# Routing six of eight expert heads in the next block: a two-layer decoder with product-key experts on one Trainium2 core

## The chip, the cores and the metric

The kernel runs on one core of one Trainium2 chip. The metric is the device time of one execution in microseconds (us), lower is better. The core's engines are PE (matrix products), DVE (vector), ACT (activations), POOL (general purpose; here it only issues the gathers) and SP (here it only issues the plain loads). They run their own instruction streams in order and meet at semaphores. Data comes from device memory over 16 DMA engines that all queues share.

## What is computed

256 tokens of width 1024 go through two layers. Each layer is a mixer (layer 0: RWKV-7 and mLSTM heads; layer 1: causal attention with forget gates, 16 heads) and then a channel mixer, which is what this case is about:

```python
def peer_ffn(x, w_q, sub_k1, sub_k2, u_tab, v_tab):      # per block of 128 tokens
    q = (xb @ w_q).reshape(T, PEER_HEADS, 2, PEER_DHALF)           # 8 heads, halves of 128
    s1 = jnp.einsum('thd,hnd->thn', q[:, :, 0], sub_k1)            # 128 scores a half
    s2 = jnp.einsum('thd,hnd->thn', q[:, :, 1], sub_k2)
    v1, i1 = lax.top_k(s1, K)                                      # K = 16
    v2, i2 = lax.top_k(s2, K)
    cand = (v1[..., :, None] + v2[..., None, :]).reshape(T, PEER_HEADS, K * K)
    sc, ci = lax.top_k(cand, K)
    eid = e1 * PEER_NKEYS + e2                                     # e1, e2: i1, i2 at ci
    gate = jax.nn.softmax(sc, axis=-1)
    act = jax.nn.gelu(jnp.einsum('td,thkd->thk', xb, u_tab[eid]), approximate=False)
    return jnp.einsum('thk,thkd->td', gate * act, v_tab[eid])
```

Every token chooses 8 x 16 = 128 experts of 16,384, and needs a row of `u_tab` and one of `v_tab` (1024 float32 each) for each. Layer norms with a scaled residual stand between all parts.

## The kernel before

**Expert blocks.** There are four: n = 2 * layer + token block, so n = 0, 1 are layer 0 and n = 2, 3 layer 1. A *row* is one expert slot s (0 to 127) for all 128 tokens of a block: one indirect DMA of POOL (line 542) gathers 128 x 2048 float32, 1 MiB, into a slot of a ring of `RING = 11`. A row then goes through four engines: DVE forms the dot product with the token (line 1700), ACT makes GELU, gate weight and a diagonal matrix of the weights (lines 1201, 1206, 1214), PE adds diagonal times v row into PSUM (line 893), and only then is the ring slot free for POOL's next gather (`pe_rows`). PE does a pair of rows one pair later than DVE (`PE_LAG = 1`).

**Routing.** `route` (lines 1644 to 1687) is DVE's work of choosing experts, for a group of two heads at a time: top 16 of four score rows, the 256 sums, top 16 of those, the indices, the softmax. It has eight hooks (`meanwhile`), at which DVE may do pairs of rows. POOL waits for `experts_chosen` (line 535) before the first row of each head; ACT's exponential (`gates`, line 1227) stands in the middle of a group, and ACT's pairs of a head wait for its `gates_ready`.

**Which block runs beside what.** The rows of a block are spread over the mixer work of another by counts of pairs, the same on DVE, ACT and PE. Block n = 0 runs beside its own routing and that of n = 1. Block n = 1 (64 pairs) runs beside the layer-1 mixer of token block b = 0: 2 + 2 pairs at its start, 16 at the sixteen weight strips of the projections (`strip_pairs`), 2 + 16 in the attention, 4 at the output projection, 3 after the norm, 1 at the queries, and then in the *tail* (`mixer1_tail`, lines 968 to 1002 on PE, 1291 to 1318 on ACT, 1788 to 1799 on DVE) 12 beside the routing of n = 2: three hooks (`tail_pairs`) in each of four groups of heads. `finish` does the 6 that are left. Block n = 2 does the same beside b = 1 and the routing of n = 3. Block n = 3 runs by itself.

**Weights.** A strip is 1 MiB of a weight matrix, 256 columns, in a ring of three (`WRING = 3`), loaded by SP (line 430) once PE has filled the PSUM bank of the strip three before. The tail's query projection (`peer_q`, line 993) takes eight strips.

**Scores.** In the tail ACT copies the scores of each group of heads to `sc[:, 0]`, which lies in memory that the next block's attention uses for `SQ`, `lg` and `probT`.

Of the kernel before, what the change touches and what calls it, by code (L numbers as in the profile page):

```python
# [77 lines left out]
def tail_pairs(g, hook):  # L78

    return int(hook in (0, 2, 5))  # L80
# [8 lines left out]
def strip_pairs(i):  # L89

    return 1
# [107 lines left out]
def build(nc, T, out):  # L199
    ROWS, NROWS = parameter_rows()  # L200
    ctx = ExitStack()
    with ctx:
# [162 lines left out]
        keyT = cut(22528, 2048).rearrange("p (i n) -> p i n", i=16)  # L365
        qT = cut(24576, 4096).rearrange("p (i n) -> p i n", i=16)
        sc = cut(28672, 4096).rearrange("p (b i n) -> p b i n", b=NB, i=16)
        cand = cut(32768, 512).rearrange("p (h n) -> p h n", h=2)
        scr = cut(33280, 512)
        onehot = cut(33792, 512).rearrange("p (h k j) -> p h k j", h=2, k=TOPK)  # L370
        v16 = cut(34304, 64).rearrange("p (i k) -> p i k", i=4)
        i16f = cut(34368, 64).rearrange("p (h two k) -> p h two k", h=2, two=2)
        csc = cut(34432, 32).rearrange("p (h k) -> p h k", h=2)
        hilo = cut(34464, 64).rearrange("p (w h k) -> p w h k", w=2, h=2)
        e12 = cut(34528, 64).rearrange("p (w h k) -> p w h k", w=2, h=2)
        eidf = cut(34592, 32)
        gate = cut(34624, NB * SLOTS).rearrange("p (b s) -> p b s", b=NB)
        hid = cut(34880, NB * SLOTS).rearrange("p (b s) -> p b s", b=NB)
        ga = cut(35136, NB * SLOTS).rearrange("p (b s) -> p b s", b=NB)
        gsum = cut(35392, 2 * EH)  # L380
        uints = cut(35408, 416).bitcast(U32)
# [4 lines left out]
        diag = [cut(35840 + j * P, P) if j < 4 else early[:, (j - 4) * P:(j - 3) * P] for j in range(DIAGS)]  # L386
        qT1 = cut(24576, 2048).rearrange("p (i n) -> p i n", i=16)
# [3 lines left out]
        ogs = cut(24576, D)  # L391
        qc = cut(25600, 1024).rearrange("p (t n) -> p t n", t=8)
        kc = cut(26624, 2048).rearrange("p (t n) -> p t n", t=8)
        fv = cut(30720, 2048).rearrange("p (b n) -> p b n", b=NB)
        SQ = cut(28672, 2048).rearrange("p (t n) -> p t n", t=16)
        lg = cut(28672, 2 * 512).rearrange("p (j q n) -> p j q n", j=2, q=2)
        probT = cut(29696, 2 * 512).rearrange("p (j q s n) -> p j q s n", j=2, q=2, s=2)
        oT = cut(32768, D).rearrange("p (t n) -> p t n", t=KT)
# [21 lines left out]
        def _(sp):  # L420
# [32 lines left out]
            load_strips(16 + 3 - 3)  # L453
            await_filled(sp, "seq_y", NCH - 1)
            load_keys(0)
            load_strips(3)
# [95 lines left out]
        def _(pe):  # L552
# [415 lines left out]
            def mixer1_tail(b, ex):  # L968
# [16 lines left out]
                for g in range(GROUPS + 1):  # L985

                    def between(j):
                        for i in (range(0, 2), range(2, 4))[j]:
                            ex.pairs(tail_pairs(g - 1, i) if g else QUERY_PAIRS * (i == 0))

                    if g < GROUPS:
                        k = EH + 1 + 4 * b + g
                        feature_strips("peer_q", k, b, between)
                        pe.wait_ge(S("peer_q_taken"), k + 1)
                        ps = claim(pe, "peer_s", k).rearrange("p (q n) -> p q n", q=4)
                        done(score_keys(ps, 0, range(4 * g, 4 * g + 4), lambda j: qT1[:, j, :]), "peer_s")
                        first_hook = 4
                    else:
                        first_hook = 0
# [21 lines left out]
        def _(act):  # L1021
# [205 lines left out]
            def gates(n, groups, meanwhile):  # L1227

                for g, (h0, h1) in enumerate(groups):
                    for i in range(6):  # L1230
                        meanwhile(g, i)
                    gates_begun[0] += 1
                    act.wait_ge(S("gate_shifted"), gates_begun[0])
                    x = gate[:, n % NB, TOPK * h0:TOPK * h1]
                    af(x, x, ACT.Exp).then_inc(S("gate_exp"), 1)
                    for i in range(6, 8):
                        meanwhile(g, i)

            def mixer1(b, ex):
                tok = slice(b * P, (b + 1) * P)  # L1240
                wide = lambda ps: ps.rearrange("p (t n) -> p t n", n=P)
                take_x(4 + 4 * b, b)
                taken(af(fz, full(act, "fox_f", b)[:, 0:P], ACT.Identity, bias=small[:, 2:3], scale=1.0), "fox_f")
                ex.pairs(EARLY_PAIRS)
                for i in range(4):
                    ex.pairs(strip_pairs(2 * i))
# [9 lines left out]
                    ex.pairs(strip_pairs(2 * i + 1))  # L1256
                for i in range(2):
                    ex.pairs(strip_pairs(8 + 2 * i))
                    taken(copy(fv[:, b, i * 512:(i + 1) * 512], full(act, "fox_v", 2 * b + i)), "fox_v")
                    ex.pairs(strip_pairs(9 + 2 * i))  # L1260
                for i in range(12, 15):
                    ex.pairs(strip_pairs(i))
                for i in range(2):
                    taken(af(ogs[:, i * 512:(i + 1) * 512], full(act, "fox_og", 2 * b + i), ACT.Sigmoid), "fox_og")
                ex.pairs(strip_pairs(15))
# [610 lines left out]
```

## Time and profile before

| | us |
|---|---|
| median of 3 runs | 1821.57 |
| lowest, highest | 1821.03, 1824.02 |
| the profiled execution, its own time | 1815.61 |
| its span, first to last instruction | 1813.6 |

| engine | busy us | share of the span |
|---|---|---|
| PE | 1551.5 | 86% |
| DVE | 1063.3 | 59% |
| ACT | 606.0 | 33% |
| POOL | 576.3 | 32% |

DMA moved 638.32 MB: 536.90 MB of gathers (512 rows) and 100.24 MB of plain loads. On the page, the chain of work that ended last is 45% PE, 32% DMA and 15% DVE. The page's strips cut the span in 40 slices of 45.3 us. In the timelines a bracket behind an instruction gives the idle time of its engine before it and what ended it; the windows give each engine's busy time in a stretch, PE's granted clock (1.00 is the full one), the DMA engines' busy share and the rate at which they moved data.

### The profile page before, as it was taken

To read this page: it belongs to the slowest core of one execution; us is meant where nothing else is said; L and a number is where in the kernel's file an instruction comes from. 1 tells how busy PE (TensorE), PEld (TensorE's weight loads), DVE (VectorE), ACT (ScalarE), POOL (GpSimd) and SP (SyncE) were. 2 spreads that over 40 slices of the span, in tenths; PEclk is the share of its full clock that TensorE was granted. 3 is DMA by queue.
4 is the path that set the end of the run, shared out by engine and by line. 5 is a ranking of instruction groups with operands and counts; after the bars stand their busy time and mean duration, and the time that the engine had idled before them with its cause. 6 is when DMAs were issued, how large, how long until landed. Compare 5 with 4: busy or idle time off the path is not lost.

```text
span 1813.6 us, 18606 instructions
## 1 busy us (share of the span) xinstructions
PE 1551.5 (86%) x6020; PEld 927.1 (51%) x6020; DVE 1063.3 (59%) x2499; ACT 606.0 (33%) x1760; POOL 576.3 (32%) x561
## 2 busy tenths in 40 slices
PE   8999988998777778997899789998999787777775
PEld 7779877664222225753457436654557433222222
DVE  1683544577888865335557984325557985444444
ACT  1434311333333333236532332246632332222222
POOL 2000000344444442333332352234542354333330
PEclk9999859999999999999999999999999899999999
DMA  6222003999999999999999989999999899999996
GB/s 245 94 93 70 1 24 126 380 413 420 419 420 419 420 420 420 419 420 420 419 418 418 407 345 419 419 419 420 419 419 419 347 357 420 420 420 420 419 421 269
DMA packets 92063, 638.32 MB, mean 352 GB/s; under 512 B 11072, under 2 KB 13120, under 8 KB 15424
## 3 DMA queue, kind: packets, MB, share of 16 engines
q0 software_dynamic: 73728, 536.90, 71.9%
q1 hardware_dynamic: 18240, 100.24, 14.1%
q8 instruction: 49, 0.80, 0.2%
q14 instruction: 46, 0.38, 0.1%
HBM read 636.05 MB, written 1.05 MB: 351 GB/s over the span
## 4 chain that ended last, share of the span: by engine, by line
PE 45%; DMA 32%; DVE 15%; ACT 6%; issue 2%; POOL 0%; ACTq 0%; SPq 0%; DVEq 0%; POOLq 0%
DMA arena<-l_peer_uv,arena 31%; PE psum L893 19%; PE psum L575 12%; DVE arena L1700 6%; PE psum L874 4%; DMA wring<-l_w_in 2%; PE psum L752 1%; PE psum L797 1%; PE psum L668 1%; DVE arena L1639 1%; DVE arena L1630 1%; PE psum L658 1%; DVE arena L1631 1%; PE psum L667 1%; DVE arena L1635 1%
## 5 line engine op out<-in xcount | busy, mean ns | idle before, releaser
L542 POOL DMA_INDIRECT arena<-l_peer_uv,arena x512 | 563.1, 1100 | 1124.8 <-PE psum L893 870.2
L1700 DVE CUSTOM_DVE_ANT_0 arena<-arena,xres 128x1024 f32<-128x1024 f32 x512 | 617.8, 1222 | 454.8 <-DMA arena<-l_peer_uv,arena 452.3
L893 PE MATMUL psum<-arena,early 128*128 128x512 f32 x1024 | 487.9, 622 | 115.5 <-ACT early L1214 112.9
L893 PE MATMUL psum<-arena 128*128 128x512 f32 x1024 | 480.7, 615 | 100.5 <-ACT arena L1214 94.7
L893 PEld LDWEIGHTS psum<-arena,early 128*128 128x128 f32 x1024 | 193.6, 197 | 380.4 <-issue 205.4
L893 PEld LDWEIGHTS psum<-arena 128*128 128x128 f32 x1024 | 192.0, 195 | 360.0 <-issue 215.8
L575 PE MATMUL psum<-xT,wring 128*128 128x128 f32 (+2 forms) x1856 | 296.5, 320 | 13.8 <-DMA wring<-l_w_in 8.4
L575 PEld LDWEIGHTS psum<-xT,wring 128*128 128x128 f32 (+1 forms) x1856 | 269.2, 191 | 55.2 <-issue 23.2
L1201 ACT ACTIVATE arena<-arena 128x2 f32<-128x2 f32 x256 | 52.0, 203 | 646.7 <-DVE arena L1700 646.4
L1206 ACT ACTIVATE arena<-arena 128x1 f32<-128x1 f32 x512 | 123.2, 287 | 24.0 <-ACT arena L1201 0.4
L1029 ACT COPY arena<-psum 128x256 f32<-128x256 f32 (+2 forms) x138 | 62.5, 472 | 192.0 <-PE psum L575 85.9
L1214 ACT ACTIVATE arena<-ident,arena 128x128 f32<-128x128 f32 x256 | 86.9, 387 | 0.0
L1214 ACT ACTIVATE early<-ident,arena 128x128 f32<-128x128 f32 x256 | 86.9, 387 | 0.0
L874 PE MATMUL psum<-wring,xT 128*128 128x256 f32 x256 | 58.2, 380 | 0.3 <-DMA wring<-l_w_in 0.2
L874 PEld LDWEIGHTS psum<-wring,xT 128*128 128x128 f32 x256 | 48.4, 190 | 14.8 <-issue 6.2
L1201 ACT ACT_TABLE_LOAD x42 | 53.9, 1283 | 0.7
L1626 DVE MAX8 arena<-arena 128x8 f32<-128x128 f32 (+1 forms) x96 | 26.1, 326 | 38.3 <-ACT arena L1029 30.9
L1700 DVE DVE_READ_ACCUMULATOR2_ANT arena<- 128x1 f32 x512 | 42.1, 82 | 0.0
L1248 ACT ACTIVATE arena<-psum 128x512 f32<-128x512 f32 x8 | 4.8, 597 | 87.8 <-PE psum L575 87.8
L1782 DVE CUSTOM_DVE_ANT_0 arena<-psum,causal_ts 128x128 f32<-128x128 f32 (+1 forms) x32 | 10.2, 355 | 40.4 <-PE psum L943 40.4
L1630 DVE FIND_INDEX8 arena<-arena 128x8 uint32<-128x128 f32 (+1 forms) x96 | 31.5, 328 | 0.0
L752 PE MATMUL psum<-wring,arena 128*128 128x256 f32 x128 | 30.9, 404 | 0.7 <-DVEq L1602 0.7
(236 smaller groups left out, 1133.9 us busy)
## 6 DMA issues: line engine op xcount, KB each, us to landing
wring<-l_w_in SPq DMA_DIRECT2D x47, 1024.0 KB
wring<-l_peer_wq SPq DMA_DIRECT2D x24, 1024.0 KB
wring<-l_w_out SPq DMA_DIRECT2D x12, 1024.0 KB
arena<-l_peer_uv,arena POOLq DMA_INDIRECT x512
ln_par<-l_ln_g SPq DMA_DIRECT2D x6, 512.0 KB
ln_par<-l_ln_b SPq DMA_DIRECT2D x6, 512.0 KB
arena<-l_peer_keys SPq DMA_DIRECT2D x2, 1024.0 KB, 7.0
xT<-x_t SPq DMA_DIRECT2D x1, 1024.0 KB, 4.9
```

The source lines that it names most:

```text
L542: pool.indirect_dma_start(out=ring[:, g % RING, :], out_offset=None, in_=T[f"l{l}_peer_uv"], in_offset=bass.IndirectOffsetOnAxis(ap=eid[:, ...
L575: last = mm(ps, w[:, k, c0:c0 + cols], xT[:, k, tok], start=(k == 0), stop=(k == KT - 1))
L752: last = mm(ps[:, b * STRIP:(b + 1) * STRIP], yT[:, k, b * P:(b + 1) * P], w[:, k, :], start=first and (b, k) == (0, ks[0]), stop=end and ...
L874: last = mm(ps[:, i * STRIP:(i + 1) * STRIP], lhs(kt), w[:, kt, :], start=(kt == 0), stop=(kt == KT - 1))
L893: last = mm(self.ps[c], diag[k % DIAGS], ring[:, g % RING, D + c * 512:D + (c + 1) * 512], start=not self.begun, stop=True, skip_group_che ...
L1029: return nc.scalar.copy(out_, in_)
L1201: af(ga[:, self.b, 2 * p:2 * p + 2], hid[:, self.b, 2 * p:2 * p + 2], ACT.Gelu).then_inc(S("gelued"), 1)
L1206: af(w, w, ACT.Copy, scale=gate[:, self.b, s:s + 1]).then_inc(S("weights"), 1)
L1214: af(diag[k % DIAGS], ident[:], ACT.Copy, scale=ga[:, self.b, s:s + 1]).then_inc(S("diags_made"), 1)
L1626: st.then(v.max(vals[:, i, 0:8], src[:, i, :]))
L1630: st.then(v.max_index(idx[:, i, 0:8], vals[:, i, 0:8], src[:, i, :]))
L1700: v.tensor_tensor_reduce(out=u, in0=u, in1=xres[:, self.b, :], scale=1.0, scalar=0.0, op0=ALU.mult, op1=ALU.add, accum_out=hid[:, self.b, ...
```

## The change

Three things are edited.

1. The tail of a block routes only the first group of the next expert block (heads 0 and 1), now with six pairs at its hooks. PE's eight strips stand there with one pair after each of the last six, and ACT takes queries and scores between pairs. So 52 pairs are done when the tail ends instead of 58, and `finish` does 12 instead of 6.
2. The other three groups (heads 2 to 7) are routed while the next expert block runs: for n = 2 beside the sixteen strips of the next mixer, where DVE's 16 pairs now stand at 16 of the 24 hooks; for n = 3 right after the layer norm, with a pair at every one of 24 hooks. ACT's three exponentials move with them.
3. The scores must outlive the attention, so they get a buffer of their own, `sc1` (2048 columns), in the place of one ring row: `RING` is 10. All other addresses stay.

```diff
+FIRST_PAIR, LATER = PAIRS[:1], PAIRS[1:]
-RING = 11
+RING = 10
-def tail_pairs(g, hook):
-    return int(hook in (0, 2, 5))
+def tail_pairs(hook):
+    return int(hook in (0, 1, 2, 4, 5, 6))
+def routed_pairs(g, hook):
+    return int((8 * g + hook) % 3 != 2)
+def pairs_before_exp(g):
+    return sum(routed_pairs(j, i) for j in range(g + 1) for i in range(8 if j < g else 6))
...
+        sc1 = behind(0, 2048).rearrange("p (i n) -> p i n", i=16)
...
-                for g in range(GROUPS + 1):
-                    def between(j):
-                        for i in (range(0, 2), range(2, 4))[j]:
-                            ex.pairs(tail_pairs(g - 1, i) if g else QUERY_PAIRS * (i == 0))
-                    if g < GROUPS:
-                        k = EH + 1 + 4 * b + g
-                        feature_strips("peer_q", k, b, between)
...
-                    if g:
-                        for i in range(first_hook, 8):
-                            ex.pairs(tail_pairs(g - 1, i))
+                pumps = iter([QUERY_PAIRS, 0] + [1] * sum(tail_pairs(i) for i in range(8)))
+                for g in range(GROUPS):
+                    k = EH + 1 + 4 * b + g
+                    feature_strips("peer_q", k, b, lambda j: ex.pairs(next(pumps)))
...
+                held = LATER if b else ()
+                def strip_step(i):
+                    ex.pairs(strip_pairs(i))
+                    for g, (h0, h1) in enumerate(held):
+                        if pairs_before_exp(g) == i + 1:
+                            gate_exp(2, h0, h1)
...
-                    taken(copy(sc[:, 0, 4 * g:4 * g + 4, :], ps), "peer_s")
+                    taken(copy(sc1[:, 4 * g:4 * g + 4, :], ps), "peer_s")
...
-                gates(2 + b, PAIRS, meanwhile)
+                gates(2 + b, FIRST_PAIR, meanwhile)
...
             ex.pairs(NEW_PAIRS)
             ln_root(6)
+            gates(3, LATER, lambda g, i: ex.pairs(1))
             ex.finish()
...
+                def meanwhile(g, i):
+                    ex.pairs(routed_pairs(g, i))
+                    if (g, i) == (0, 4):
+                        decay_sizes()
+                if b:
+                    route(1, 0, LATER, meanwhile)
+                else:
+                    for i in range(16):
+                        ex.pairs(strip_pairs(i))
+                        if i == 2:
+                            decay_sizes()
...
-                route(1, b, PAIRS, lambda g, i: ex.pairs(tail_pairs(g, i)))
+                route(1, b, FIRST_PAIR, lambda g, i: ex.pairs(tail_pairs(i)))
...
             layer_norm(6)
+            route(1, 1, LATER, lambda g, i: ex.pairs(1))
             ex.finish()
```

On PE, in the tail of token block 0, from the second group of strips on. Line 575 is a strip of `peer_q`, 893 a row pair, 815 the scores of a group. Before:

```order
L575 MATMUL psum<-xT,wring 128x128 x16
L893 MATMUL psum<-arena 128x512 x4
L575 MATMUL psum<-xT,wring 128x128 x16
L893 MATMUL psum<-arena,early 128x512 x4
L815 MATMUL psum<-arena 128x128 x4
L893 MATMUL psum<-arena,early 128x512 x4
L575 MATMUL psum<-xT,wring 128x128 x16
L893 MATMUL psum<-arena 128x512 x4
L575 MATMUL psum<-xT,wring 128x128 x16
L893 MATMUL psum<-arena 128x512 x4
L815 MATMUL psum<-arena 128x128 x4
L893 MATMUL psum<-arena 128x512 x4
```

And in the changed kernel, where these lines are 588, 906 and 828:

```order
L588 MATMUL psum<-xT,wring 128x128 x16
L906 MATMUL psum<-arena 128x512 x4
L588 MATMUL psum<-xT,wring 128x128 x16
L906 MATMUL psum<-arena,early 128x512 x4
L828 MATMUL psum<-arena 128x128 x4
L588 MATMUL psum<-xT,wring 128x128 x16
L906 MATMUL psum<-arena,early 128x512 x4
L588 MATMUL psum<-xT,wring 128x128 x16
L906 MATMUL psum<-arena 128x512 x4
L828 MATMUL psum<-arena 128x128 x4
```

The pair behind each group's scores is gone: two pairs a group instead of three.

On DVE, at the end of the first routed group in the same tail (1681 to 1686 are its last operations, 1626 begins the next group, 1700 a row's dot product). Before:

```order
L1681 SCALAR_TENSOR_TENSOR arena<-arena 128x32
L1682 CAST arena<-arena 128x32
L1684 TENSOR_REDUCE arena<-arena 128x2
L1685 RECIPROCAL arena<-arena 128x2
L1686 TENSOR_TENSOR arena<-arena 128x32
L1626 MAX arena<-arena 128x8 x4
L1700 ISA arena<-arena,xres 128x1024
```

And in the changed kernel, where 1716 is the dot product; 24 rows follow, and then the layer norm:

```order
L1697 SCALAR_TENSOR_TENSOR arena<-arena 128x32
L1698 CAST arena<-arena 128x32
L1700 TENSOR_REDUCE arena<-arena 128x2
L1701 RECIPROCAL arena<-arena 128x2
L1702 TENSOR_TENSOR arena<-arena 128x32
L1716 ISA arena<-arena,xres 128x1024
L1716 ISA arena 128x1
```

Three groups of head routing have left this place.

## Rows read from the trace of the kernel before

**Rows 1.** The page's section 2: GB/s in 40 slices of 45.3 us.

```profile
GB/s 245 94 93 70 1 24 126 380 413 420 419 420 419 420 420 420 419 420 420 419 418 418 407 345 419 419 419 420 419 419 419 347 357 420 420 420 420 419 421 269
```

**Rows 2.** Windows: length; PE, PEld, DVE, ACT, POOL busy; clock, DMA share, GB/s.

```profile
440.00:640.00 200.00, 148.61 (x312) 58.00 (x312) 166.49 (x478) 61.17 (x210) 86.52 (x79) 0.97 1.01 420
...
1040.00:1072.00 32.00, 25.57 (x46) 10.37 (x45) 30.04 (x75) 12.88 (x43) 12.43 (x11) 0.82 0.82 304
...
1120.00:1200.00 80.00, 80.00 (x357) 54.42 (x356) 25.73 (x41) 18.51 (x69) 23.64 (x23) 1.00 1.01 419
...
1424.00:1480.00 56.00, 42.06 (x84) 17.70 (x83) 52.15 (x151) 20.05 (x62) 25.06 (x19) 0.85 0.84 309
...
1560.00:1760.00 200.00, 148.01 (x320) 57.49 (x320) 98.64 (x160) 50.68 (x201) 75.14 (x81) 1.00 1.01 420
```

**Rows 3.** DVE's timeline, two group starts; the tail's window for line 1700.

```profile
1011.64 0.87 DVE L1626 MAX8 arena<-arena 128x8 f32<-128x128 f32 x4
...
1034.24 0.86 DVE L1626 MAX8 arena<-arena 128x8 f32<-128x128 f32 x4
...
966.40:1056.80 90.40, 28.33 (x48) 0.92 0.98 398
```

**Rows 4.** POOL's gathers and a DVE dot product in the timeline of the first hole.

```profile
1042.59 0.94 POOL L542 DMA_INDIRECT arena<-l_peer_uv,arena  x1 [9.01 <-PE psum L893]
...
1066.53 1.50 POOL L542 DMA_INDIRECT arena<-l_peer_uv,arena  x1 [1.94 <-PE psum L893]
...
1072.86 1.23 DVE L1700 CUSTOM_DVE_ANT_0 arena<-arena,xres 128x1024 f32<-128x1024 f32 x1 [2.20 <-DMA arena<-l_peer_uv,arena]
```

**Rows 5.** Dots and loads by line, 944.7-1073.5/937-1073, then 1224.2-1479.3/1211-1475.

```profile
L1700 DVE CUSTOM_DVE_ANT_0 arena<-arena,xres x41: 1204/1221/1226, 944.8 to 1072.9; 128x1024 f32<-128x1024 f32 x41
L430 SPq DMA_DIRECT2D wring<-l_peer_wq x5: 328/328/1095, 964.0 to 995.2; - x5
L430 SPq DMA_DIRECT2D wring<-l_w_in x2: 337/385/433, 1013.6 to 1014.0; - x2
L430 SPq DMA_DIRECT2D wring<-l_w_in_rest x1: 555/555/555, 996.6 to 996.6; - x1
995.61 0.43 SPq L446 DMA_DIRECT2D ln_par<-l_ln_g  x1
L1700 DVE CUSTOM_DVE_ANT_0 arena<-arena,xres x86: 1204/1221/1236, 1224.3 to 1479.2; 128x1024 f32<-128x1024 f32 x86
L430 SPq DMA_DIRECT2D wring<-l_peer_wq x8: 327/380/912, 1328.6 to 1401.1; - x8
L430 SPq DMA_DIRECT2D wring<-l_w_out x3: 327/328/432, 1211.2 to 1328.2; - x3
1401.46 0.43 SPq L446 DMA_DIRECT2D ln_par<-l_ln_g  x1
```

**Rows 6.** Timelines of POOL and DVE early in block 0.

```profile
371.94 0.94 POOL L542 DMA_INDIRECT arena<-l_peer_uv,arena  x1 [8.01 <-PE psum L893]
...
378.14 1.22 DVE L1700 CUSTOM_DVE_ANT_0 arena<-arena,xres 128x1024 f32<-128x1024 f32 x1
...
380.87 1.23 DVE L1700 CUSTOM_DVE_ANT_0 arena<-arena,xres 128x1024 f32<-128x1024 f32 x1 [1.50 <-DMA arena<-l_peer_uv,arena]
```

**Rows 7.** PE's timeline in the tail: a strip, a pair of rows, the scores.

```profile
973.03 3.84 PE L575 MATMUL psum<-xT,wring 128*128 128x128 f32 x32 [0.27 <-DMA wring<-l_peer_wq]
976.70 3.60 PE L893 MATMUL psum<-arena,early 128*128 128x512 f32 x8
980.14 1.05 PE L815 MATMUL psum<-arena 128*128 128x128 f32 x8
```

**Rows 8.** One row's dot product on DVE, and the gather that its release lets go.

```profile
1147.30 1.23 DVE L1700 CUSTOM_DVE_ANT_0 arena<-arena,xres 128x1024 f32<-128x1024 f32 x1 [2.20 <-DMA arena<-l_peer_uv,arena]
...
1171.58 0.94 POOL L542 DMA_INDIRECT arena<-l_peer_uv,arena  x1 [4.23 <-PE psum L893]
```

More of the change, by code:

```diff
@@ L372, in build @@
[L372 to L379, printed above, removed]
@@ new lines, in build @@
+        onehot = behind(13312, 512).rearrange("p (h k j) -> p h k j", h=2, k=TOPK)
+        v16 = behind(13824, 64).rearrange("p (i k) -> p i k", i=4)
+        i16f = behind(13888, 64).rearrange("p (h two k) -> p h two k", h=2, two=2)
+        csc = behind(13952, 32).rearrange("p (h k) -> p h k", h=2)
+        hilo = behind(13984, 64).rearrange("p (w h k) -> p w h k", w=2, h=2)
+        e12 = behind(14048, 64).rearrange("p (w h k) -> p w h k", w=2, h=2)
+        eidf = behind(14112, 32)
+        gate = behind(14144, NB * SLOTS).rearrange("p (b s) -> p b s", b=NB)
@@ L382, in build @@
+        hid = behind(14400, NB * SLOTS).rearrange("p (b s) -> p b s", b=NB)
+        ga = behind(14656, NB * SLOTS).rearrange("p (b s) -> p b s", b=NB)
+        gsum = behind(14912, 2 * EH)
+        uints = behind(14928, 416).bitcast(U32)
         i16 = uints[:, 0:64].rearrange("p (i k) -> p i k", k=TOPK)
@@ L385, in build @@
         eid = uints[:, 160:416].rearrange("p (b s) -> p b s", b=NB)
[L386 to L398, printed above, removed]
+        diag = [behind(15360 + j * P, P) if j < 4 else early[:, (j - 4) * P:(j - 3) * P] for j in range(DIAGS)]
+        qT1 = behind(4096, 2048).rearrange("p (i n) -> p i n", i=16)
+        ogs = behind(4096, D)
+        qc = behind(5120, 1024).rearrange("p (t n) -> p t n", t=8)
+        kc = behind(6144, 2048).rearrange("p (t n) -> p t n", t=8)
+        fv = behind(10240, 2048).rearrange("p (b n) -> p b n", b=NB)
+        SQ = behind(8192, 2048).rearrange("p (t n) -> p t n", t=16)
+        lg = behind(8192, 2 * 512).rearrange("p (j q n) -> p j q n", j=2, q=2)
+        probT = behind(9216, 2 * 512).rearrange("p (j q s n) -> p j q s n", j=2, q=2, s=2)
+        oT = behind(12288, D).rearrange("p (t n) -> p t n", t=KT)
         fz, fl, fc = mr[:, 0, 0:P], mr[:, 0, P:SEQ], mr[:, 1, :]
@@ L452, in _ @@
             load_ln(0)
-            load_strips(16 + 3 - 3)
+            load_strips(16 + WRING - 3)
             await_filled(sp, "seq_y", NCH - 1)
             load_keys(0)
-            load_strips(3)
+            load_strips(6 - WRING)
             load_ln(2)
@@ L1245, in mixer1 @@
                 for i in range(4):
-                    ex.pairs(strip_pairs(2 * i))
+                    strip_step(2 * i)
                     ps = wide(full(act, "fox_qk", 4 * b + i))
@@ L1305, in take_scores @@
                     ps = full(act, "peer_s", EH + 1 + 4 * b + g).rearrange("p (q n) -> p q n", q=4)
-                    taken(copy(sc[:, 0, 4 * g:4 * g + 4, :], ps), "peer_s")
+                    taken(copy(sc1[:, 4 * g:4 * g + 4, :], ps), "peer_s")
+                taking = iter([(take_queries, 1), (take_scores, 1), (take_queries, 2), (take_scores, 2), (take_queries, 3),
+                               (take_scores, 3)])
                 def meanwhile(g, i):
-                    ex.pairs(tail_pairs(g, i))
-                    if g + 1 < GROUPS and i == 1:
-                        take_queries(g + 1)
-                    if g + 1 < GROUPS and i == 3:
-                        take_scores(g + 1)
+                    if tail_pairs(i):
+                        ex.pairs(1)
+                        take, g = next(taking)
+                        take(g)
                 ex.pairs(QUERY_PAIRS)
@@ L1746, in mixer1, with decay_sizes @@
             def mixer1(b, ex):
-                for i in range(2):
-                    ex.pairs(strip_pairs(i))
-                dve.wait_ge(S("fox_f_taken"), b + 1)
-                stt(fl, fz, -1.0, fz, ALU.mult, ALU.max).then_inc(S("f_abs"), 1)
-                for i in range(2, 16):
-                    ex.pairs(strip_pairs(i))
+                def decay_sizes():
+                    dve.wait_ge(S("fox_f_taken"), b + 1)
+                    stt(fl, fz, -1.0, fz, ALU.mult, ALU.max).then_inc(S("f_abs"), 1)
+                def meanwhile(g, i):
[9 more added lines that the diff above has]
+                            decay_sizes()
                 ex.pairs(RMS_PAIRS)
```

46 lines of the change are left out of this document (21 added, 25 removed).

## The prediction

> **What bounds the kernel now.** Read the page's GB/s line first [rows 1]: from slice 8 (363 us) on it stands at 418 to 421, with two holes, slices 22 and 23 (407, 345) and slices 31 and 32 (347, 357). The windows say the same at closer range: the DMA engines are busy 1.01 of the time and move 420 GB/s in the stretch of block 0 (440 to 640 us), 419 beside the mixer's strips (1120 to 1200) and 420 where block 3 runs alone (1560 to 1760); between 1040 and 1072 us they move 304, between 1424 and 1480 us 309 [rows 2]. So from 363 us to the last row the bytes of gathers and weights set the time, and only those two holes are open to gain. A row of 1 MiB costs 1.0486 MB / 420 GB/s = 2.50 us, a pair 5.0, a strip another 2.5.
>
> What makes a hole: POOL's gathers there wait for PE's line 893, that is for a ring slot to come free, once for 9.01 us [rows 4]. PE's rows wait for DVE. In the first hole DVE is busy for 30.04 of 32 us [rows 2]. It routes: one group of two heads takes 1034.24 - 1011.64 = 22.6 us [rows 3] and lets 3 pairs pass. In that time DMA needs 6 rows and 2 strips = 8 x 2.50 = 20.0 us. The ring covers the shortfall for about three groups, then DMA has nothing queued. At the end DVE has a stock of landed rows that it works off at 1.22 us a row, until it waits for DMA again at 1072.86 [rows 4].
>
> **Term 1, the holes.** By bytes: 32 x (420 - 304) / 420 = 8.8 us and 56 x (420 - 309) / 420 = 14.8 us, together 23.6 [rows 2]. But the end hangs on when whole rows have landed, and a row has landed when the last of 16 engines is through, so a second count goes from one dot product that waited for its row to the next such one [rows 5]. First hole: 41 dots from 944.77 to 1072.86 us are 40 rows; 5 + 2 strips and half a strip (the rest of w_in) are issued between, one more was under way, and the norm's parameters are another MiB: 49.5 MiB x 2.50 = 123.8 us in 128.1 us, 4.3 idle. Second: 85 rows, 11 strips, 1 for the norm: 97 x 2.50 = 242.5 us in 254.8 us, 12.3 idle. Together 16.6. The bounds are thus 16.6 and 23.6; I take **20**, between them, since either count has a reason and no row decides.
>
> **What the change does to the tail.** DVE: a group without its rows costs 22.6 minus its share of line 1700, 28.33 / 4 = 7.1, so 15.5 us [rows 3]; its six rows are that 7.1. With six pairs it costs 15.5 + 14.2 = 29.7 us, and DMA needs 12 x 2.50 = 30.0 us for the rows alone and another 20 for eight strips. DVE is no longer late: the 12 pairs left are then taken as they land. That removes the cause of both holes. Who is late next is PE. A strip costs it about 3.7 us, a pair 3.6, the scores 1.05 [rows 7]. A group of two strips with two pairs is 7.4 + 7.2 + 1.05 = 15.7 us, against 4 rows and 2 strips = 15.0 us of DMA. Three such groups fall behind by 2 us, and the rows stand behind two strips of which the last is loaded only once the bank three strips before it is full. Bounds for the idle time that this makes: 0, if what the ring holds covers it, and 5 us a tail (the 2 us and one wait such as the 2.5 us that a strip's own transfer takes). The second tail starts with less in the ring, so I take 1 us there and 0 in the first.
>
> **What it does to the next mixer (n = 2).** DVE gets 3 x 15.5 = 46.5 us of routing. The sixteen strip steps need 16 x 3 x 2.50 = 120 us of DMA, and DVE is busy there 25.73 of 80 us [rows 2], some 39 of 120; with the routing 85 of 120. It fits. No row shows routing in this stage, so from both sides: it costs nothing as long as a dot that comes late by the routing between two pairs does not hold PE. That is at most about 6 us: 15.5 us over eight hooks is 1.9 each, and up to three such pieces stand together where hooks have no pair. PE is busy 80.00 of 80 us here and runs behind DVE: the row dotted at 1147.30 freed its slot for the gather at 1171.58, 24 us later [rows 8], of which the dot is 1.2 and the pair's matmuls 3.6 [rows 7]. ACT's part is in the rest, but with PE never idle most of it is standing in line before PE; I count 15 us as cover for the 6, so the cost is 0. If the cover were gone, 16 pairs late by up to 2.9 us each are the 46.5. PE's strips wait for nothing new. ACT's three exponentials stand before a pair of strips each and wait for DVE's shifted scores; behind them on ACT stand the squares and copies of the attention's queries, and PE waits for these only when four banks later. DVE in its turn waits for the exponential at the end of a group, where ACT has just come from a PSUM bank of PE's: one or two us, under the same cover.
>
> POOL is held at the first row of heads 2 and 3, row 32. It may ask for it when row 22 is released; DVE has these heads chosen with 10 pairs done, 20 rows. So `experts_chosen` never holds a gather, nor for later heads (15 pairs done, row 64 wanted after 54).
>
> **Block 3.** Three groups with 8 pairs each: 15.5 + 16 x 1.18 (28.33 us / 24 rows, [rows 3]) = 34.4 us of DVE against 16 x 2.50 = 40 us of DMA. The trace has just this: block 0 beside the routing of block 1, DVE 166.49 of 200 us busy and 420 GB/s [rows 2]. Cost 0. The last rows, the layer norm and the store are as before.
>
> **The ring of ten.** With ten slots row r is asked for when row r + 1 was before. That matters only where a row came close. With an empty queue a gather needs 1072.86 - 1066.53 = 6.3 us from issue to dot [rows 4]. Early in block 0 the gather issued at 371.94 was dotted at 380.87, and the one before it would now be issued at 371.94 and is wanted at 378.14: 6.2 us [rows 6]. So it is tight but just in time there, with a strip under way besides. Elsewhere the ring loses one row of eleven. Bounds 0 and 2.5 us at each of about four places where PE is held up by other work (that one, the end of each attention, the start of the mixer). I take 1 us in all.
>
> By the Trainium skill, "DMA: Bandwidth & Descriptors", the section on the anatomy of a DMA by the GpSimd path, such a transfer takes 2.0 us plus its bytes at 436 GB/s, an estimate of 4.4 us for a row, and by that the ring would have 2 us more to spare at every tight place and cost nothing. The trace does not agree (6.3 us with the issue), so its figure is used.
>
> **The sum.** -20 + 1 + 1 = **-18 us**. Against the profiled execution's own 1815.6 us (1.99 us outside the span stay) that is 1797.6. It lay 6.0 us under the median of the runs; the same step below 1821.6 gives **1803.6 us**, 0.99 of before.
>
> **The rivals.**
> *A part of the hole stays (1811).* In the tail PE is the late one by 5 us each time, and the ring of ten loses 2.5 us at two places: of the 18 us gained 7 to 12 are given back, say 1811. For it: PE's 15.7 against 15.0 us, and that gathers are now asked for later. Against: PE has 1.4 us a pair to spare in the 12 pairs that follow.
> *All bytes come back (1798).* The GB/s count is the right one: -23.6. It is the low end of the range.
> *Nothing is gained (1820).* The idle time only moves: DVE's stalls in the mixer make the 15 us of cover vanish and the holes open there, about as large. It needs PE to lose its backlog; PE busy 80.00 of 80 us speaks against it.
> *Slower (1850).* The routing stands in series in the mixer of n = 2. One mechanism: DVE routes, a landed row waits, PE has no backlog, each strip step gets longer than 7.5 us. Price 3 x 15.5 = 46.5 less 18, so 1850. It begins where a row's whole turn (landing, DVE, ACT, PE, release, new gather) exceeds ten rows' worth of this stage, 10 x 3.75 = 37.5 us: 24 us after the dot and 6.3 to land are 31, and up to 6 of routing make 37. That is near, which is why the case has a chance at all; but the 24 us are mostly backlog and shrink when DVE is late.
> The Trainium skill has a rule that speaks for this side: "SBUF — State Buffer", section on the two separate sides, says that while DVE runs certain copies GpSimd is locked out of a port and cannot write the descriptors of its DMAs, so that the DMA starves. In the windows POOL is busy 86.52 us for 79 gathers beside routing and 75.14 us for 81 without [rows 2], 0.17 us more for each, and DMA stays at 420. For the 64 rows or so beside moved groups that is 11 us of POOL's time, none of it on the path.
>
> **Chances.** Forecast and its neighbour at 1798: 0.72. Part of the hole stays: 0.16. Nothing gained: 0.07. Slower: 0.05. What a measurement of this kernel can tell from no change is about 0.2%, 3.6 us: faster 0.88, same 0.07, slower 0.05. The range from 1797 to 1812 holds the first two cases, with the bounds of term 1 and the costs of ring and PE.
>
> **What would show it.** In the changed kernel's GB/s line the two holes are gone and no slice between 363 us and the last row is under 410. DVE's dots of n = 1 and n = 2 wait for DMA right after the single group in the tail. In the mixer of token block 1 DVE is busy some 28 of 40 us and GB/s stays at 419. The first gather of heads 2 and 3 waits for PE and not for DVE. Wrong would be: POOL waiting for DVE's line of chosen experts; PE idle for ACT's diagonals between strips; a hole at 1390 to 1420 us, where PE works off strips in the second tail.

## The result

| | us |
|---|---|
| before, median of 4 runs (range) | 1821.30 (1819.67 to 1824.02) |
| changed, median of 4 runs (range) | 1805.45 (1804.22 to 1809.39) |
| ratio, with its 95% interval | 0.9915 (0.9895 to 0.9936) |
| the profiled execution of the change, its span | 1806.65, 1804.5 |

The change saves 15.9 us; 18 were forecast. The repeats below gave 0.9928 (0.9913 to 0.9942) and 0.9912 (0.9893 to 0.9931), 13.8 and 16.0 us, so the three medians put the saving at 14 to 16 us.

### The profile page after: what moved, and what is told of

It reads as the page before. It is cut to its first block, busy times and chain, and to the rows that moved or that the text cites. A ratio compares the mean times of both kernels' runs of the same rounds, so it can differ in the third digit from the quotient of the medians.

```text
span 1804.5 us, 18617 instructions
## 1 busy us (share of the span) xinstructions
PE 1544.5 (86%) x6020; PEld 925.0 (51%) x6020; DVE 1063.3 (59%) x2499; ACT 604.9 (34%) x1759; POOL 579.8 (32%) x561
## 4 chain that ended last, share of the span: by engine, by line
PE 49%; DMA 37%; DVE 6%; ACT 5%; issue 2%; POOL 1%; ACTq 0%; SPq 0%; POOLq 0%; DVEq 0%
DMA arena<-l_peer_uv,arena 34%; PE psum L906 21%; PE psum L588 14%; PE psum L887 4%; DVE arena L1716 3%; DMA wring<-l_w_in 2%; PE psum L765 1%; DMA wring<-l_peer_wq 1%; PE psum L681 1%; PE psum L810 1%; PE psum L671 1%; PE psum L680 1%; ACT L1203 1%; POOL arena L555 1%; ACT early L1216 1%
## 5 line engine op out<-in xcount | busy, mean ns | idle before, releaser
L906 PE MATMUL psum<-arena,early 128*128 128x512 f32 x1024 | 477.8, 611 | 105.8 <-ACT early L1216 105.8
L906 PEld LDWEIGHTS psum<-arena,early 128*128 128x128 f32 x1024 | 189.4, 193 | 365.4 <-issue 194.6
L588 PE MATMUL psum<-xT,wring 128*128 128x128 f32 (+2 forms) x1856 | 296.5, 320 | 13.6 <-DMA wring<-l_w_in 8.4
L1031 ACT COPY arena<-psum 128x256 f32<-128x256 f32 (+2 forms) x138 | 62.5, 471 | 222.6 <-PE psum L588 125.8
L1647 DVE MATCH_REPLACE8 arena<-arena 128x128 f32<-128x128 f32 (+1 forms) x96 | 30.7, 320 | 0.0
L1456 DVE SCALAR_TENSOR_TENSOR arena<-psum,pars,arena 128x255 f32<-128x255 f32 x14 | 6.8, 482 | 40.2 <-ACT arena L1055 40.2
```

The costliest lines, as they stand in the source:

```text
L588: last = mm(ps, w[:, k, c0:c0 + cols], xT[:, k, tok], start=(k == 0), stop=(k == KT - 1))
L906: last = mm(self.ps[c], diag[k % DIAGS], ring[:, g % RING, D + c * 512:D + (c + 1) * 512], start=not self.begun, stop=True, skip_group_che ...
L1031: return nc.scalar.copy(out_, in_)
L1647: st.then(v.match_replace(scratch[:, i, :], vals[:, i, 0:8], src[:, i, :], -BIG))
```

## The profile after

Engines' busy time from the page's first section, then its GB/s line in 40 slices of 45.1 us, to be laid beside [rows 1]:

```profile
PE 1544.5 (86%) x6020; PEld 925.0 (51%) x6020; DVE 1063.3 (59%) x2499; ACT 604.9 (34%) x1759; POOL 579.8 (32%) x561
...
GB/s 246 95 92 72 1 11 130 342 390 419 419 420 419 420 420 413 419 419 420 419 415 419 414 420 416 420 419 420 419 378 419 405 420 421 419 420 420 420 419 260
```

DVE's total is the same to the tenth: no work was saved, only moved. The two deep holes of before (407, 345 and 347, 357) are gone. Three shallow ones are there: 390 in slice 8, 378 in slice 29, 405 in slice 31. The page's chain of work that ended last is now 49% PE, 37% DMA and 6% DVE, where DVE had 15%. The windows of the changed kernel (length; PE, PEld, DVE, ACT, POOL busy; clock, DMA share, GB/s) give first the place of the old first hole, then the new ones at close range:

```profile
1040.00:1072.00 32.00, 23.81 (x51) 9.24 (x50) 14.80 (x24) 7.72 (x30) 12.96 (x13) 0.97 1.01 420
376.00:384.00 8.00, 8.00 (x20) 3.56 (x19) 5.39 (x16) 4.48 (x19) 4.90 (x5) 1.00 0.80 264
1320.00:1328.00 8.00, 8.00 (x31) 5.54 (x30) 2.19 (x4) 2.47 (x10) 1.88 (x2) 1.00 0.62 224
1328.00:1336.00 8.00, 8.00 (x31) 5.54 (x30) 5.96 (x10) 1.50 (x7) 3.38 (x2) 1.00 1.00 374
1416.00:1424.00 8.00, 7.73 (x24) 3.82 (x23) 7.51 (x16) 5.84 (x19) 4.31 (x4) 1.00 0.97 376
1424.00:1432.00 8.00, 8.00 (x20) 3.61 (x19) 3.67 (x7) 2.14 (x9) 5.36 (x6) 1.00 0.98 385
```

Where [rows 2] had DVE busy for 30.04 of 32 us and 304 GB/s, DVE now is busy for 14.80 and the DMA engines for all of it. DVE's timeline in the first tail shows the turn. It finishes its one group, waits for ACT's exponential, works off five landed rows, and from then on waits for DMA before every row:

```profile
1014.02 0.19 DVE L1700 TENSOR_REDUCE arena<-arena 128x2 f32<-128x32 f32 x1 [8.28 <-ACT arena L1242]
...
1014.55 1.22 DVE L1716 CUSTOM_DVE_ANT_0 arena<-arena,xres 128x1024 f32<-128x1024 f32 x1
...
1019.13 1.22 DVE L1716 CUSTOM_DVE_ANT_0 arena<-arena,xres 128x1024 f32<-128x1024 f32 x1
...
1021.21 1.22 DVE L1716 CUSTOM_DVE_ANT_0 arena<-arena,xres 128x1024 f32<-128x1024 f32 x1 [0.85 <-DMA arena<-l_peer_uv,arena]
...
1072.21 1.23 DVE L1716 CUSTOM_DVE_ANT_0 arena<-arena,xres 128x1024 f32<-128x1024 f32 x1 [1.27 <-DMA arena<-l_peer_uv,arena]
1074.70 1.23 DVE L1716 CUSTOM_DVE_ANT_0 arena<-arena,xres 128x1024 f32<-128x1024 f32 x1 [1.26 <-DMA arena<-l_peer_uv,arena]
```

The last two stand 2.49 us apart, one row at the full rate. The 8.28 us are a new wait, three rows long. The rows that piled up were worked off at 1.15 us each, and DMA moved 406 and 410 GB/s in the two windows of 8 us from 1008 us on, so the wait cost half a us of bytes at most.

Now the next mixer. First for the kernel before, its window of 1080 to 1200 us and DVE's longest sum of waits in it (us in total, times, longest); then both for the changed kernel:

```profile
1080.00:1200.00 120.00, 116.43 (x518) 77.25 (x517) 48.44 (x78) 31.07 (x107) 38.47 (x36) 0.97 1.01 420
```

```profile
DVE arena L1700 <- DMA arena<-l_peer_uv,arena: 70.9, 31, 3.8
```

```profile
1080.00:1200.00 120.00, 114.44 (x518) 76.46 (x518) 84.92 (x254) 36.97 (x113) 38.80 (x34) 0.99 1.01 418
```

```profile
DVE arena L1716 <- DMA arena<-l_peer_uv,arena: 34.6, 21, 3.8
```

The routing went into time in which DVE waited for DMA: 36.5 us more work in this window, 36.3 us less waiting, and still 34.6 us to spare.

**Stretch by stretch.** The dot products of line 1716 (1700 before) are counted through, 512 of them; row 217 is the first that waits in the tail's approach to the first hole, row 348 the first dot product in the second tail's routing, row 384 the first of block 3. Times from one to the next, us, one trace of each kernel:

| kernel | first gather at | to row 44 | 44 to 217 | 217 to 256 | 256 to 264 | 264 to 348 | 348 to 384 | 384 to end |
|---|---|---|---|---|---|---|---|---|
| before | 321.0 | 136.3 | 492.1 | 123.4 | 20.7 | 279.5 | 106.1 | 334.5 |
| changed | 324.4 | 139.3 | 490.9 | 120.1 | 19.9 | 279.8 | 94.9 | 335.1 |
| a1_changed | 321.0 | 136.5 | 491.7 | 120.0 | 20.0 | 279.2 | 94.9 | 335.7 |
| c1_changed | 327.0 | 138.6 | 491.3 | 120.1 | 19.9 | 279.3 | 95.1 | 335.5 |
| a2_ring11 | 327.1 | 136.1 | 491.2 | 121.3 | 19.9 | 279.3 | 95.1 | 335.7 |
| c2_ring11 | 324.6 | 136.2 | 492.1 | 120.1 | 20.0 | 279.3 | 95.2 | 335.7 |
| a3_old_ring10 | 324.6 | 138.9 | 491.5 | 126.6 | 19.9 | 278.2 | 108.5 | 335.2 |
| a4_ring9 | 321.1 | 139.0 | 492.8 | 120.0 | 20.0 | 279.4 | 97.1 | 334.5 |
| b1_only_first | 323.5 | 136.2 | 492.1 | 120.1 | 20.0 | 279.4 | 109.1 | 335.0 |
| b2_only_second | 324.3 | 136.3 | 492.3 | 125.8 | 20.0 | 279.0 | 96.3 | 333.9 |
| b3_routing_plus_31 | 323.8 | 136.2 | 492.1 | 120.0 | 19.9 | 280.8 | 95.1 | 336.6 |
| b4_routing_plus_62 | 324.5 | 138.6 | 491.4 | 120.0 | 19.9 | 307.9 | 95.7 | 333.9 |

From the first gather on, the changed kernel's trace is 12.6 us shorter than that of before: 3.0 lost up to row 44, 1.2 won behind it, 15.0 won from row 217 to 384 (3.3 in the first hole, 0.8 behind it, 11.2 in the second, -0.3 between), 0.6 lost at the end. The span shrank by only 9.1, because the first gather came 3.5 us later, in layer 0, which the change does not touch. The "first gather at" column moves between 321 and 327 us in code that is the same up to there. Of the 7.7 us between the spans of the three traces of the changed kernel (1799.2 to 1806.9), 6.0 lie ahead of the first gather. The profiled execution of before was an early one.

## The experiments

Each carries a ratio to runs of the kernel before on the same chip. Their medians there were 1818.17 for the a set, 1818.82 for b and 1819.91 for c.

**Is the ring's lost row part of the price?** The changed kernel again, with eleven rows, with nine, and the old order with ten. With eleven rows the scores of all four groups lie elsewhere, in memory that costs no ring row; otherwise only the number of rows changes, and all other addresses stay.

```diff
-RING = 10
+RING = 11
...
+        def scores1(g):
+            if g == 0:
+                return sc[:, 0, 0:4, :]
+            if g < 3:
+                return masks[:, 512 * (g - 1):512 * g].rearrange("p (i n) -> p i n", i=4)
+            return mr[:, 4:6, :].rearrange("p r (i n) -> p (r i) n", i=2)
```

> The changed kernel again, as the yardstick for the kernels timed beside it. Both theories: ratio to before 0.991, some 16 us less. Holes in the DMA rate at about 376 to 384 us and 1320 to 1328 us, of 3 and 4 us.

Measured: 1804.42 us, 0.9928 (0.9913 to 0.9942). The hole at 1320 us came again (378 in slice 29), the one at 376 us did not (415 GB/s in that window).

> The moved routing with all eleven ring rows: the scores of heads 2 to 7 lie in tiles that layer 1 leaves unused (1024 columns of the masks, 512 of the small rows), so no ring row is given up. Theory 1 (the ring of ten costs 7 us, at 376 and at 1320 us, because a gather issued one release later comes late): 7 us less than the changed kernel, ratio to before 0.987, both holes gone, the small one at 1416 to 1432 us smaller. Theory 2 (what idle time is left comes from the new order of work, or from the start of the run): within 2 us of the changed kernel.

Measured: 1801.27 us, 0.9913 (0.9898 to 0.9928), 3.1 us less than a1: under half of what theory 1 said, and a little over theory 2. Of the two holes the one at 376 us is gone (394 GB/s) and the one at 1320 us is not (396 in slice 29).

> The kernel before with ten ring rows and nothing else. Theory 1: the same two new holes (3 and 4 us) and up to 2.5 us more in each old one: 7 to 12 us slower than before, ratio 1.004 to 1.007. Theory 2: no difference, under 2 us.

Measured: 1820.30 us, 1.0016 (1.0002 to 1.0030), 2.1 us more than before. Theory 1 named 7 to 12 and two new holes, of which only the one at 376 us came (255 GB/s; 417 in slice 29); the median lies just over theory 2.

> The changed kernel with nine ring rows, all else in place. Theory 1: each place where PE is held up loses 2.5 us more, and places that just held with ten begin to lose (starts of the mixers, the second tail): 12 to 20 us slower than the changed kernel. Theory 2: the ring is no limit, under 5 us slower.

Measured: 1807.02 us, 0.9948 (0.9933 to 0.9962), 2.6 us more than a1, as theory 2 said.

The changed kernel with eleven rows seemed 3.1 us faster, in a trace that is not shorter from the first gather on (1478.7 against 1478.2 us). So the pair was run once more.

> Repeat, beside the next kernel, of the changed kernel: ratio 0.9928 as measured in the first set.

Measured: 1803.91 us, 0.9912 (0.9893 to 0.9931).

> Repeat of the moved routing with all eleven ring rows. The first set gave 3 us less than the changed kernel by the medians, with intervals that touch, and no difference from the first gather to the end of the two traces. If the eleventh row is worth what the medians said: again 2 to 4 us less, ratio 0.991. If the traces are right: within 1.5 us of the changed kernel.

Measured: 1805.10 us, 0.9925 (0.9907 to 0.9943).

Now eleven rows were 1.2 us slower, within the 1.5 us that stood for the traces being right. The two pairs give 1 us in the mean for the eleventh row, with 3.1 and -1.2 apart: less than these runs can tell. In the table it seems to show in one place: up to row 44 all three traces with eleven rows take 136.1 to 136.3 us, while of eight with ten rows four take 138.6 to 139.3. Where such a trace shows a hole, it is in the window at 376 us above; three traces with eleven rows are too few to be sure of it. Nine rows cost 2.6 us by medians whose intervals overlap, and the table shows 2.2 us in the second tail, 97.1 instead of 94.9.

The hole at 1320 us is not the ring's. Slice 29 reads 360 to 396 in all nine traces with the first tail moved, with nine, ten and eleven rows, and 416 to 419 in the three without.

The old order reacts otherwise. With ten rows its first hole grew from 123.4 to 126.6 us and its second from 106.1 to 108.5, and these are its windows at the two holes, against 304 and 309 GB/s in [rows 2]:

```profile
1040.00:1072.00 32.00, 20.77 (x34) 8.51 (x35) 31.35 (x95) 10.56 (x34) 8.08 (x8) 0.79 0.78 302
1424.00:1480.00 56.00, 39.91 (x88) 17.87 (x87) 54.66 (x175) 19.19 (x58) 14.99 (x14) 0.79 0.80 302
```

A ring row is stock for the time in which DVE falls behind. With one row less the stretch of each open hole is 2.4 to 3.2 us longer, about one row's 2.5 us, here and in b1 and b2 below. Where the holes are closed, the tails show no such loss from eleven rows to ten. The medians are less sharp: the lost row costs 2.1 us in the old order, with an interval that reaches to 5.5, and 1 us in the new one. (The trace of a3 is 6.4 us longer from the first gather on, but it is of one of its slower executions, 1825.94 us, and 2.6 us of that lie ahead of row 44.) So that the row was dear in the old kernel and is nearly free in the new one is what the stretches say; the medians don't contradict it and don't prove it.

**Which half does it?** One tail keeps the old order with all four groups in it, the other has the new one. Both have ten rows.

```diff
+MOVED = (0,)
...
-                held = LATER if b else ()
+                held = LATER if b and 0 in MOVED else ()
...
-                pumps = iter([QUERY_PAIRS, 0] + [1] * sum(tail_pairs(i) for i in range(8)))
+                if b in MOVED:
+                    pumps = iter([QUERY_PAIRS, 0] + [1] * sum(tail_pairs(i) for i in range(8)))
...
+                for g in range(GROUPS + 1):
```

> Ten rows; only the first tail (token block 0) hands six heads on to the next mixer, the second routes all eight in place as before. Theory rows (a hole costs what the landings of whole rows lose: 3.4 us in the first, 12.6 in the second): 3 us gained less what the ring gives up (3 us in the kernel before with ten rows): ratio 0.998 to 1.002. Theory bytes (a hole costs the bytes not moved, 8.8 and 14.8 us): 8.8 less 3, ratio 0.997.

Measured: 1818.09 us, 0.9997 (0.9982 to 1.0012). That is theory rows; the 0.997 of theory bytes lies outside the interval.

> Ten rows; only the second tail hands six heads on, to block 3 which runs by itself. Theory rows: 12.6 us gained, less up to 3 for the ring in the first hole: 10 to 12 us, ratio 0.993 to 0.9945, nearly all that the whole change brings. Theory bytes: 14.8 less 3, and clearly less than the whole change.

Measured (`MOVED = (1,)`): 1810.13 us, 0.9947 (0.9929 to 0.9966), 8.7 us less than before: somewhat under both theories, and within the interval it can't tell them apart.

GB/s of both, first b1, then b2:

```profile
GB/s 244 94 93 70 1 24 116 370 414 419 420 419 420 419 420 407 419 420 420 419 416 417 413 420 419 419 420 419 420 378 419 336 348 420 421 419 420 420 420 272
```

```profile
GB/s 245 94 94 71 1 23 119 349 415 419 419 420 419 420 419 397 419 420 419 420 420 419 414 332 420 419 419 420 419 416 419 397 420 420 420 420 420 420 420 267
```

Each half closes its own hole and leaves the other, which is now deeper (336 and 348 for 347 and 357; 332 for 345), as in a3, whose ring is as short (341 and 353; 339). The stretches add up. Against the old order with ten rows the first tail is worth 126.6 - 120.1 = 6.5 us and the second 108.5 - 94.9 = 13.6; against eleven rows 3.3 and 11.2. Moving the first alone wins 3.3 us, loses 3.0 in the second hole (109.1 for 106.1) and so comes out at nothing. The first half of this change, tried alone, would have looked worthless. What no run separates is the routing from PE's new order in the same tail: both moved together each time.

**How near is the mixer's limit?** The rival "slower" said that the routing would stand in series there. To find the point from which that is so, DVE does more routing at the same place: the top 16 of each moved group's score rows are taken two or four times more, with the same values.

```diff
+                    for _ in range(2 if extra else 0):
+                        top16(sc1[:, js, :], scratch[:, 0:2 * nh, :], v16[:, 0:2 * nh, :], i16[:, 0:2 * nh, :], 2 * nh,
+                              lambda: None)
```

> The changed kernel; in the mixer of block 2 each of the three groups does the top 16 of its four score rows twice more (same values again), 5.2 us each time by the durations of the rows, 31 us of DVE in all. Theory cover (DVE has 120 - 85 = 35 us free there and PE's backlog hides when a dot comes late): 0 to 3 us slower than the changed kernel. Theory series (the moved routing is on the path in this stage, and what the holes gave was partly spent there): 15 to 31 us slower.

Measured: 1806.28 us, 0.9928 (0.9908 to 0.9949).

> The same with four repeats, 62 us more of DVE: more than the stage has free. Theory cover: now DVE sets the stage; 147 us of work against 120, 20 to 35 us slower than the changed kernel. Theory series: 62 us slower.

Measured: 1834.66 us, 1.0087 (1.0069 to 1.0104).

DVE's busy time on the two pages is 29.6 and 58.4 us above the changed kernel's 1063.3:

```profile
PE 1545.0 (86%) x6020; PEld 923.5 (51%) x6020; DVE 1092.9 (61%) x2691; ACT 605.3 (34%) x1759; POOL 579.0 (32%) x561
```

```profile
PE 1548.3 (85%) x6020; PEld 926.1 (51%) x6020; DVE 1121.7 (61%) x2883; ACT 605.3 (33%) x1759; POOL 583.2 (32%) x561
```

Both came out as theory cover had it. The first 29.6 us cost about nothing: the ratio is that of a1, and rows 264 to 348 take 280.8 us for 279.2 to 279.8 in the changed kernel and its repeats. The next 28.8 cost 27.1 us in the same stretch. Windows, first of b3, then of b4:

```profile
1120.00:1160.00 40.00, 39.76 (x205) 27.61 (x204) 36.15 (x147) 14.40 (x45) 10.71 (x12) 1.00 1.01 419
1160.00:1200.00 40.00, 37.58 (x126) 24.13 (x125) 38.60 (x157) 10.09 (x30) 11.49 (x12) 0.96 1.01 419
```

```profile
1120.00:1160.00 40.00, 31.09 (x164) 21.57 (x164) 39.10 (x155) 11.62 (x35) 9.90 (x9) 0.91 0.85 331
1160.00:1200.00 40.00, 31.58 (x116) 20.10 (x115) 38.94 (x178) 9.86 (x29) 9.52 (x9) 0.87 0.89 359
```

In b3 DVE is busy for up to 38.60 of 40 us and DMA still runs at 419: this is the edge. In b4 DVE is full, and the wait goes round: DVE is late, so ACT's diagonals are, so PE's rows, so POOL's gathers. These are one wait of PE and one of POOL in b4's timelines, and DVE's waits for DMA, which are nearly gone (34.6 us in the changed kernel):

```profile
1134.61 5.31 PE L906 MATMUL psum<-arena,early 128*128 128x512 f32 x8 [8.90 <-ACT early L1216]
...
1138.47 0.94 POOL L555 DMA_INDIRECT arena<-l_peer_uv,arena  x1 [15.13 <-PE psum L906]
```

```profile
DVE arena L1719 <- DMA arena<-l_peer_uv,arena: 7.7, 5, 2.2
```

So the rival's mechanism exists, its place is right, and its point is where DVE's own work fills the stage. 84.9 + 58.4 = 143.3 us of work against 120 us of DMA leaves 23 us in series; 28.1 were measured over the changed kernel's 279.8, and the runs don't say where the other 5 come from. The change stands some 30 us of DVE work on the near side of it.

## Why the prediction was right, and where not

**The bound and what lifts it: right in the main.** DVE's routing made the holes, and with one group in each tail they close; b1 and b2 show it hole by hole. The time is inside the range, 1.9 us above the number. By the stretches, 15.0 us come from rows 217 to 384, that is from the two places named. Two readings were too simple. Slice 8 of [rows 1] stands at 413, not at 418 or more. And DMA does not set the time everywhere from 363 us on: from row 331 to row 348, at the end of the attention and in the output projection, the dot products take 64.4 to 64.9 us in before, changed, a3, b1 and b2 alike, whether or not DMA has a hole there, and PE is busy for 24.00 of 24 us from 1320 to 1344 us in before and in the changed kernel.

That the number came so near is in part luck. From the first gather on, the traces of the changed kernel are 12.6, 12.7 and 14.4 us shorter than the one of before: the holes gave less than forecast (15.3 for 20), the start of block 0 could lose more (3.0 for 1), and up to 3.3 us of the medians' difference stand in no stretch.

**Term 1, the size: too large.** This is the term that was mis-sized: 20 us forecast, 15.3 measured. Two counts stood for the two holes, 23.6 us by missing bytes and 16.6 by landed rows, and 20 was taken between them because "no row decides". The stretches say 3.3 + 0.8 + 11.2 = 15.3 us, with what the ring and the new order give back in it; the row count (4.3 and 12.3) is right to about a microsecond for each. The byte count overstates both, and the traces hold a likely reason. Each row's transfer raises its semaphore once for each of the 16 DMA engines: the changed kernel's trace has 16 records for every one of its 512 rows. The times of the first and the last of these, us, read from the semaphores' records:

```
kernel   row   first     last      apart
before   230    979.59    992.80  13.21
before   247   1038.76   1048.01   9.25
before   252   1055.88   1060.52   4.65
before   255   1068.58   1069.21   0.62     behind the first hole
before   368   1421.47   1425.10   3.63
before   377   1453.51   1454.01   0.49     in the second hole
changed  339   1321.97   1329.53   7.56
changed  340   1329.79   1332.03   2.24     in the hole at 1320 us
changed  342   1340.38   1341.44   1.06
```

So the 16 engines do not keep step: at row 247, as the first hole begins, the last was 9.25 us, nearly four rows, behind the first. A reading that fits all this: when the gathers stop, the engines that are ahead run dry while the others still work. Their idle time counts in GB/s, but a row has landed only with the last engine, so a hole first uses up this lead. The two counts differ by 4.5 us where the engines stood 9.25 apart and by 2.5 where they stood 3.6 apart: the order fits; that it is half the distance each time is a guess.

The lead also goes with the hole at 1320 us. POOL waits 10.19 us for PE there in both kernels, at the end of the attention, but at row 330 the records lie 7.6 to 10.4 us apart in the changed kernel, its repeats, a2, c2 and b1, which have the hole, and 2.0 to 2.9 us in before, a3 and b2, which do not. Nine rows (a4) lie between with 5.3 us and have the hole; b4 has it with 2.2 us, so the lead is not the only way to it. The wait of before, then of the changed kernel:

```profile
1323.32 0.94 POOL L542 DMA_INDIRECT arena<-l_peer_uv,arena  x1 [10.19 <-PE psum L893]
```

```profile
1324.72 0.94 POOL L555 DMA_INDIRECT arena<-l_peer_uv,arena  x1 [10.19 <-PE psum L906]
```

By its two windows this hole lacks 8 x (196 + 46) / 420 = 4.6 us of bytes. From row 259 to row 347, which waited for their data in before and in the changed kernel, the dot products take 275.9 us before and 278.3 changed: the data come 2.4 us later. Yet rows 264 to 348 take 279.5 and 279.8 us. Row 348 had landed 13.6 and 11.4 us before its dot product began; DVE waited for scores, which come from PE by way of ACT, and PE is busy 50.29 us from 1320 to 1373 us in both. First before, then changed:

```profile
1372.23 0.87 DVE L1626 MAX8 arena<-arena 128x8 f32<-128x128 f32 x4 [14.01 <-ACT arena L1029]
```

```profile
1373.63 0.87 DVE L1642 MAX8 arena<-arena 128x8 f32<-128x128 f32 x4 [11.87 <-ACT arena L1031]
```

So this hole was free because PE set the time where it fell, and not because holes are.

Of the two counts the row count was the one to take, and the sum would then have been -14.6 us, with 14 to 16 measured. The lead of the engines could have been read from the trace of before, which would have spoken against the byte count.

**The tail.** That DVE is no longer late is shown by its timeline. That PE is the late one in the second tail is shown too: the "hole at 1390 to 1420 us" named as a sign of error came, small, at 1416 to 1432 us, 376 and 385 GB/s, 8 x (44 + 35) / 420 = 1.5 us for the 1 us taken. PE's timeline there is the alternation that was worked out, without a gap:

```profile
1403.05 3.74 PE L588 MATMUL psum<-xT,wring 128*128 128x128 f32 x32
1406.63 3.60 PE L906 MATMUL psum<-arena 128*128 128x512 f32 x8
1410.06 3.73 PE L588 MATMUL psum<-xT,wring 128*128 128x128 f32 x32
1413.63 3.60 PE L906 MATMUL psum<-arena,early 128*128 128x512 f32 x8
1417.07 1.05 PE L828 MATMUL psum<-arena 128*128 128x128 f32 x8
```

Not seen beforehand was ACT: DVE waits 8.28 us for the exponential in the first tail and 10.33 in the second, where the prediction had no wait. Its "one or two us" was for the same wait in the mixer, where DVE's list of waits shows none.

**The mixer: 0 was right.** The GB/s stay at 418. Rows 264 to 348 take 0.3 us more in the profile of the change, 0.3 and 0.2 less in its repeats. DVE was to be busy 85 of 120 us and was 84.92, but that agreement is luck: both terms of the 85 missed by some 10 us, in opposite directions. Before, DVE was busy 48.44 us there and not 39, since the window's first 13 us hold a layer norm and rows that are worked off; and 36.5 us came on top and not 46.5, in part since the last of the routing falls behind 1200 us. As for the cover: one hook's piece being hidden by PE's backlog was not tested by itself, but b3 puts some 10 us of routing (29.6 / 3) without a pair into each of the three groups, and these were hidden as well. The 15 us of cover were enough, and what limits the stage in b4 is DVE's total, not the delay of a single row.

The Trainium skill, "SBUF — State Buffer", section on the two separate sides, says that a DVE copy of the right kind locks GpSimd out and starves the DMAs that it issues. None of it is seen with this routing: in b3 DVE is busy 38.60 of 40 us beside gathers, and DMA moves 419 GB/s. POOL's whole busy time is 576.3 us before, 579.8 changed and 576.9 in its first repeat, over 512 gathers.

**Block 3: 0, right** within 1 us (334.5 before, 335.1 to 335.7 after); whether the routing there costs that microsecond the runs do not settle, for b2, which has it too, took 333.9.

**The ring: 1 us, about right**, and in the place named, as far as the runs can tell. The gather that was "tight but just in time" is the one below, and it is not always in time: the stretch up to row 44 loses 2.4 to 3.1 us in four of eight traces with ten rows, 1.4 in the mean of the eight. That the same lost row costs 5.6 us by the stretches where both holes stay open was not thought of; with the first tail alone moved, it ate the gain.

```profile
377.50 1.91 POOL L555 DMA_INDIRECT arena<-l_peer_uv,arena  x1 [7.99 <-PE psum L906]
```

**POOL's new wait: as said.** From 363 us to the end POOL waited for PE and for nothing else that has a name, not for the chosen experts:

```profile
POOL arena L555 <- PE psum L906: 833.5, 434, 10.2
POOL arena L555 <- issue: 26.4, 64, 2.2
```

**The step to the median.** The prediction laid the same 6.0 us between the profiled execution and the median on both sides. But the profiled execution of before had an early first gather (321.0 us) and that of the change a later one (324.4), so the two profiled times differ by 9.0 us and the medians by 15.9. The first number alone would have told a wrong story.

**A sign that was wrongly set.** "No slice under 410" failed three times (390, 378, 405) in a kernel in which the holes are closed. It would have called a right theory wrong. The rival "a part of the hole stays" was drawn too narrow as well: 7 to 12 us given back are 1811 to 1816 us, and only the low end got a number.

## What to carry to other kernels

When transfers bound a stage and an engine falls behind in one place, move its work to where it waits for those transfers, and check the sum of its work there against the stage's transfer time: here, in b3, it fitted up to 38.60 of 40 us. Price a hole in the transfer rate by the time between two consumers that waited for their data, less the bytes between them at full rate, and not by the bytes missing in it; then see whether the next thing that ends a wait is such a consumer at all. Judge a buffer row and the removal of the stall that it covers together: here either alone read wrong.

## What the hardware showed

The 16 DMA engines drift apart under a steady load of rows cut over all of them. The first and the last semaphore record of a row lie 2.5 us apart in rows 49 to 59 of the changed kernel (1.8 to 3.5 in the other traces), 13.21 us at row 230 of before, and 0.4 to 0.8 us at rows 375 to 378 of before, where the queue had run empty. The byte rate in a window and the time at which rows have landed then tell different things: two holes of 8.8 and 14.8 us by bytes were 4.3 and 12.3 us by landed rows.

The first gather came at 321, 324 or 327 us (321.0 to 321.1, 323.5 to 324.6, 327.0 to 327.1) behind identical code of layer 0, in steps of some 3 us. No run here shows why. A difference below that step is better read from a stretch behind it than from the whole time.
